# Decoder attention: the third bank of turned probabilities goes from VectorE to ScalarE

## The chip, the cores and the metric

The kernel runs on one core of a Trainium2 chip. The metric is the device time of one execution in microseconds: 2270.2 us is the median of three (2270.14 to 2271.83). The profile is of one more execution, which took 2272.19 us; its instructions span 2270.4 us.

## The reference

Two blocks of a decoder over 512 tokens of width 1024, in float32. The change lies in the attention of the second block, whose core is, with 16 heads in 2 groups of 8 and 64 columns a head:

```
scale = HEAD_DIM ** -0.5
s = einsum('bghqd,bgnd->bghqn', q_c, k_cmp) * scale - slopes * dist     # 31 compressed keys
o_cmp = softmax(s) @ v_cmp
s = einsum('bghqd,bgqkld->bghqkl', q_c, ks) * scale - slopes * dist     # selected blocks
o_slc = softmax(s) @ vs
s = einsum('bghqd,bgmd->bghqm', q_c, kw) * scale - slopes * dist        # window of 512
o_win = softmax(s) @ vw
o = g_c[0] * o_cmp + g_c[1] * o_slc + g_c[2] * o_win                    # gates, per token and head
out = o @ w_out
```

With 512 tokens all 8 blocks of 64 are selected and the window of 512 reaches over all earlier tokens, so the second and the third softmax are both causal over all keys and differ in their keys and values.

## The kernel before, in words

All matrices stand as 128 partitions by columns. Weights are streamed from memory, and each product of float32 values is made of three matmuls on rounded high and low parts (`products`, L288 to L290). They are most of the kernel. The attention (`attend_tensor`, `attend_scalar`, `attend_vector`) is one stage of some 210 us out of 2270.

The attention works on **pairs** of heads, one of each group, 8 pairs in all. A turn of its loop holds 2 pairs, and there are 4 turns. A pair is 5 items, in the list `ITEMS`: item 0 the compressed keys, items 1 and 2 the selected keys for group 0 and 1, items 3 and 4 the window keys for group 0 and 1. In a turn the second pair's items are numbered 5 to 9. For each item but the compressed one:

- TensorE makes the scores (`scores_tensor`, L1965) in banks 2, 3 and 4 of PSUM (the accumulators).
- VectorE reads them, adds the bias by distance and finds the extreme value of each row (`read_vector`, L2155), four pieces of 512, 384, 128 and 256 columns into `Pr`.
- ScalarE takes the exponential of each piece with its row sum (`exp_scalar`, L2067).
- VectorE inverts the sums, multiplies with the gate and scales the probabilities (`scale_vector`, L2190, L2193, L2198).
- TensorE turns (transposes) them, ten 128x128 blocks into banks 5, 6 and 1 (`turn_probs_tensor`, L1991), and raises `turned` after each bank.
- The three banks are evicted into `PT[g]`, 512, 512 and 256 columns: banks 5 and 1 by ScalarE (`evict_scalar`, L2081, `pT_act`), bank 6 by VectorE (`evict_vector`, L2166, `pT_dve`).
- After the second group's item (2 and 4) TensorE multiplies values with both `PT`, 16 matmuls (`weigh_tensor`, L2010), here called the **weighing**. It waits for the evictions. So does the next turning, since it writes the same banks.

In between TensorE makes the query projection of the pair after next (`pair_tensor`, with `products`), two of eight chunks at a time. When it is complete, ScalarE evicts its high parts (`q_scalar`, L2090, `q_high`) and VectorE makes its low parts (`q_vector`, L2129, `q_ready`). This stands behind item 1's eviction on ScalarE and behind item 2's scaling on VectorE, once a pair, except where no pair follows. GpSimd splits one weight tile a pair meanwhile (L233, L253).

Each engine runs its own instructions strictly in the order in which the functions below write them. ScalarE's step n is: exponentials of item n+2, eviction of item n, then `q_scalar` at items 1 and 6. VectorE's step n is: scores of item n+2, eviction of item n, scaling of item n+1, then `q_vector`. TensorE's step n is: turning of item n, a part of a projection, scores of item n+3, weighing.

Of the kernel before, what the change touches and what calls it, by code (L numbers as in the profile page):

```python
# [136 lines left out]
def program(nc, t, out):  # L137

    with ExitStack() as ctx:
# [4 lines left out]
        def at(name, offset, cols, dt=F32, parts=P):  # L144
            return nc.alloc_sbuf_tensor_at(name, [parts, cols], dt, offset=base + offset)
# [37 lines left out]
        bank = [ctx.enter_context(nc.psum_tensor(f"bank{i}", [P, 512], F32)) for i in range(8)]  # L183

        def sem(name):
            return ctx.enter_context(nc.semaphore(name))
# [22 lines left out]
        def wait_apart(engine, semaphore, value):  # L209


            engine.wait_ge(semaphore, value)
            engine.sem_inc(passed, 1)
# [1596 lines left out]
        def kv_vector(dve, order):  # L1810
# [58 lines left out]
            for i in range(2):  # L1869
# [27 lines left out]
        PR_OF = [0, 1, 2, 0, 1, 2, 0, 1]  # L1897
        PT = [at("PT0", 42 * KB, PCOLS), at("PT1", behind_r, PCOLS)]
        (alibi_ready, c_scored, scores_read, piece_read, c_maxed, c_shifted, probs_done, c_summed, c_turned, cT_ready, scored,
         turned, pT_act, pT_dve, inverse, weight_ready, probs_scaled, q_high, q_ready, pair_done, y_high, y_low) = (  # L1900
            sem(n) for n in ("alibi_ready c_scored scores_read piece_read c_maxed c_shifted probs_done c_summed c_turned cT_ready "
                             "scored turned pT_act pT_dve inverse weight_ready probs_scaled q_high q_ready pair_done y_high y_low").split())
        q_units, q_tiles = seg_a.unit0 + 7, seg_a.tile0 + 7
        TURNS = NQ // 2
        Q_PARTS = {2: (0, 2), 3: (2, 4), 4: (4, 6), 0: (6, 8)}
# [1 line left out]
        def item(idx):  # L1907

            return ITEMS[idx % N_ITEMS]

        def nth(i, idx):

            return i * N_ITEMS + idx

        def s_nth(i, idx):

            return i * 8 + (idx // N_ITEMS * 8 + sum(1 for it in ITEMS[:idx % N_ITEMS] if it[1]))

        def c_nth(i, idx):

            return i * 2 + (idx // N_ITEMS * 2 + sum(1 for it in ITEMS[:idx % N_ITEMS] if not it[1]))

        def probs(idx):
            return Pr[PR_OF[sum(1 for it in ITEMS[:idx % N_ITEMS] if it[1])]]
# [44 lines left out]
        def turn_probs_tensor(pe, i, idx):  # L1969

            _, r, g = item(idx)
            if r:
                pe.wait_ge(probs_scaled, nth(i, idx) + 1)
            else:
                wait_apart(pe, probs_scaled, nth(i, idx) + 1)
                for b in range(NB):
                    mm = nc.tensor.transpose(bank[5][0:64, b * P:(b + 1) * P], Pc[:, b * 64:(b + 1) * 64], ident)
                mm.then_inc(c_turned, 1)
                return
            if g:  # L1980
                pe.wait_ge(pT_dve, s_nth(i, idx))
                pe.wait_ge(pT_act, s_nth(i, idx) * 2)
            elif r == 1:
                pe.wait_ge(cT_ready, c_nth(i, idx))
            P_ = probs(idx)
            for pieces, (first, _), into in zip(TURNED, GROUPS, (bank[5], bank[6], bank[1])):
                for kb, col in pieces:
                    for b in range(kb, NB):
                        at0 = col - first + (b - kb) * P
                        c = WHERE[b] + kb * P  # L1990
                        mm = nc.tensor.transpose(into[:, at0:at0 + P], P_[:, c:c + P], ident)  # L1991
                mm.then_inc(turned, 1)

        def weigh_tensor(pe, i, idx):

            j, r, g = item(idx)
            if r == 0:
                pe.wait_ge(y_low, i * 2 + (j + 1))
                pe.wait_ge(cT_ready, c_nth(i, idx) + 1)
                nc.tensor.matmul(bank[7][:, :], v_cmp[:, :], PcT[:, :], start=True, stop=False)  # L2000
                return
            if g == 0:
                return
            m = s_nth(i, idx)
            pe.wait_ge(pT_dve, m + 1)
            pe.wait_ge(pT_act, m * 2 + 2)
            for kb in range(NB):
                col = KEYS_AT[kb]
                for e in range(2):
                    mm = nc.tensor.matmul(bank[7][HALVES[e], kb * P:], v_tok[r - 1][:, kb * P + 64 * e:kb * P + 64 * e + 64],  # L2010
                                          PT[e][:, col:col + (NB - kb) * P], start=False, stop=r == 2 and kb == NB - 1)
            if r == 2:
                mm.then_inc(pair_done, 1)
# [57 lines left out]
        def evict_scalar(act, i, idx):  # L2071

            _, r, g = item(idx)
            if r == 0:
                act.wait_ge(c_turned, c_nth(i, idx) + 1)
                nc.scalar.activation(PcT[:, :], bank[5][0:64, :], ACT.Identity).then_inc(cT_ready, 1)
                return
            for n, source_bank in ((0, bank[5]), (2, bank[1])):
                act.wait_ge(turned, s_nth(i, idx) * 3 + (n + 1))
                first, end = GROUPS[n]  # L2080
                nc.scalar.activation(PT[g][:, first:end], source_bank[:, 0:end - first], ACT.Identity).then_inc(pT_act, 1)  # L2081
# [50 lines left out]
        def read_vector(dve, i, idx):  # L2132


            _, r, g = item(idx)
            V = nc.vector
            if r == 0:
                c = c_nth(i, idx)
                dve.wait_ge(alibi_ready, c * 4 + 2)
                dve.wait_ge(c_scored, c + 1)  # L2140
                V.tensor_tensor(Pc[:, :], bank[2][:, 0:2 * P], alibi_c[:, :], ALU.add).then_inc(scores_read, 1)
                dve.wait_ge(scores_read, nth(i, idx) + 2)
                by_block = Pc[:, :].rearrange("p (b n) -> p b n", n=32)
                V.tensor_reduce(c_max, by_block, AX.X, ALU.max).then_inc(c_maxed, 1)
                dve.wait_ge(c_maxed, c + 1)
                V.tensor_tensor(by_block, by_block, over_columns(c_max, 32), ALU.subtract).then_inc(c_shifted, 1)
                return
            if r == 1:
                dve.wait_ge(alibi_ready, c_nth(i, idx) * 4 + (g - 1))
            P_ = probs(idx)  # L2150
            for n, pieces in enumerate(PIECES):
                wait_apart(dve, scored, s_nth(i, idx) * 3 + (n + 1))
                for b, col in pieces:
                    at0 = col - GROUPS[n][0]
                    ins = V.tensor_tensor_reduce(P_[:, col:col + (b + 1) * P], bank[2 + n][:, at0:at0 + (b + 1) * P],  # L2155
                                                 alibi[g][:, (3 - b) * P:], -KEY_SCALE, 3.0e38, ALU.add, ALU.min,
                                                 stat(idx, 0)[:, b:b + 1])
                ins.then_inc(piece_read if n < 2 else scores_read, 1)

        def evict_vector(dve, i, idx):  # L2160

            _, r, g = item(idx)
            if r:
                m = s_nth(i, idx)
                dve.wait_ge(turned, m * 3 + 2)
                nc.vector.tensor_copy(PT[g][:, 512:1024], bank[6][:, :]).then_inc(pT_dve, 1)  # L2166

        def scale_vector(dve, i, idx):

            j, r, g = item(idx)  # L2170
# [37 lines left out]
        def attend_vector(dve):  # L2208
            nc.vector.sem_inc(scores_read, 1)
            nc.vector.sem_inc(y_low, 1)  # L2210
            nc.vector.sem_inc(tile_taken, NQ)
            read_vector(dve, 0, 0)
            read_vector(dve, 0, 1)
            scale_vector(dve, 0, 0)

            def turn(i):
                for n in range(N_ITEMS):
                    if exists(i, n + 2):
                        read_vector(dve, i, n + 2)
                    evict_vector(dve, i, n)  # L2220
                    if exists(i, n + 1):
                        scale_vector(dve, i, n + 1)
                    if n % PER_PAIR == 1 and exists(i, n + PER_PAIR - 1):
                        q_vector(dve, *((i, 1) if n < PER_PAIR else (i + 1, 0)))
                    if n == PER_PAIR:
                        y_vector(dve, i, 0)
                    if n == 0 and not (isinstance(i, int) and i == 0):
                        y_vector(dve, i - 1, 1)

            turn(0)  # L2230
            with dve.Fori(1, TURNS - 1) as i:
                turn(i)
            turn(TURNS - 1)
            y_vector(dve, TURNS - 1, 1)
# [224 lines left out]
```

## Time and profile before

| | |
|---|---|
| median of three runs | 2270.2 us (2270.14 to 2271.83) |
| profiled execution | 2272.19 us, its span 2270.4 us |
| TensorE busy | 2129.6 us, 94% |
| VectorE busy | 1186.0 us, 52% |
| ScalarE busy | 851.5 us, 38% |
| GpSimd busy | 778.0 us, 34% |
| mean granted TensorE clock | 0.972 of full speed |
| chain of work that ended last | TensorE 79%, VectorE 11%, issue 5%, ScalarE 4% |

Whole-kernel shares say little on the attention. There the rows by stage, by line and in order of time have to be read: which instruction on TensorE waits, for whom, and what that engine did just before.

### The profile page before, as it was taken

The page shows a single profiled execution, that of the slowest core. Times are in us where ns is not written, and L with a number is a line of the kernel's source. Part 1 is how long each engine was busy: PE and PEld are TensorE (multiplying, and loading weights), DVE is VectorE, ACT ScalarE, POOL GpSimd, SP SyncE. Part 2 cuts the span into 40 slices and gives each one's busy share as a digit, 9 for nine tenths or more (in the row PEclk, how much of TensorE's full clock was granted, in tenths as well). Part 3 has the DMA queues.
Part 4 walks back from the last instruction along what each step waited for, and adds up shares of the span by engine and source line. Part 5 has one row for each costly group of instructions (what it writes and reads, how often), then busy time and mean ns, then how long its engine had stood idle before and what let it go on. Part 6 is the DMA issues. An engine that isn't in the chain of part 4 may idle for free.

```text
span 2270.4 us, 32867 instructions
## 1 busy us (share of the span) xinstructions
PE 2129.6 (94%) x11670; PEld 1714.6 (76%) x11670; DVE 1186.0 (52%) x1862; ACT 851.5 (38%) x1516; POOL 778.0 (34%) x336
## 2 busy tenths in 40 slices
PE   3889999989899999899979999999999989999997
PEld 2768788768688888768757888888877667888886
DVE  6476977762533332289964333323677864333323
ACT  3333442433432332275543232322366643323221
POOL 2632332404244444300114444444411114444442
PEclk8989999999999999999989999999999999999999
DMA  3311211203233332211113333322200003333332
GB/s 120 102 56 42 63 38 40 64 2 120 66 101 92 101 102 98 70 56 47 56 28 93 93 101 92 129 93 87 71 20 19 28 22 92 100 92 101 102 102 75
DMA packets 43652, 168.98 MB, mean 74 GB/s; under 512 B 4848, under 2 KB 4912, under 8 KB 43056
## 3 DMA queue, kind: packets, MB, share of 16 engines
q1 hardware_dynamic: 43056, 163.59, 23.6%
q10 hardware_dynamic: 512, 4.24, 0.5%
q8 instruction: 56, 0.92, 0.2%
q14 instruction: 28, 0.23, 0.0%
HBM read 165.72 MB, written 2.10 MB: 74 GB/s over the span
## 4 chain that ended last, share of the span: by engine, by line
PE 79%; DVE 11%; issue 5%; ACT 4%; POOL 1%; DMA 1%; DVEq 0%; ACTq 0%; POOLq 0%; SPq 0%
PE bank L288 21%; PE bank L289 21%; PE bank L290 21%; PE bank L745 2%; PE bank L2010 2%; PE bank L1965 1%; DVE act_q L1019 1%; POOL WL L253 1%; PE bank L1507 1%; PE bank L1509 1%; PE bank L1508 1%; ACT Pr L2067 1%; PE bank L1991 1%; DVE ACC L415 1%; PE bank L314 1%
## 5 line engine op out<-in xcount | busy, mean ns | idle before, releaser
L253 POOL TENSOR_TENSOR WL<-raw,WR 128x1024 fp32r<-128x1024 f32 (+2 forms) x274 | 713.0, 2602 | 1031.1 <-ACT WR L249 1026.5
L288 PE MATMUL bank<-XR,WR 128*128 128x512 f32 x1528 | 616.6, 404 | 28.6 <-DVE XL L444 19.5
L290 PE MATMUL bank<-XR,WL 128*128 128x512 f32 x1528 | 597.4, 391 | 0.0
L289 PE MATMUL bank<-XL,WR 128*128 128x512 f32 x1528 | 597.1, 391 | 0.0
L249 ACT ACTIVATE WR<-raw 128x1024 fp32r<-128x1024 f32 (+2 forms) x230 | 256.0, 1114 | 781.3 <-PE bank L290 772.2
L288 PEld LDWEIGHTS bank<-XR,WR 128*128 128x128 f32 x1528 | 288.5, 189 | 103.8 <-issue 33.6
L288 PE MATMUL bank<-MR,WR 128*128 128x512 f32 (+1 forms) x856 | 338.2, 395 | 13.6 <-DVE ML L1678 6.1
L289 PEld LDWEIGHTS bank<-XL,WR 128*128 128x128 f32 x1528 | 288.7, 189 | 65.2 <-issue 8.3
L290 PEld LDWEIGHTS bank<-XR,WL 128*128 128x128 f32 x1528 | 288.1, 189 | 61.0
L289 PE MATMUL bank<-ML,WR 128*128 128x512 f32 (+1 forms) x856 | 333.1, 389 | 0.0
L290 PE MATMUL bank<-MR,WL 128*128 128x512 f32 (+1 forms) x856 | 333.0, 389 | 0.0
L233 POOL CAST WR<-raw 128x1024 fp32r<-128x1024 f32 (+1 forms) x58 | 64.9, 1118 | 436.9 <-PE bank L290 377.1
L1463 DVE TENSOR_TENSOR f_up<-bank,R 128x512 f32<-128x512 f32 x66 | 45.6, 692 | 306.0 <-PE bank L290 306.0
L288 PEld LDWEIGHTS bank<-MR,WR 128*128 128x128 f32 x856 | 163.3, 191 | 52.0 <-issue 12.1
L290 PEld LDWEIGHTS bank<-MR,WL 128*128 128x128 f32 x856 | 163.6, 191 | 33.0
L289 PEld LDWEIGHTS bank<-ML,WR 128*128 128x128 f32 x856 | 163.9, 191 | 31.1 <-issue 0.2
L415 DVE TENSOR_TENSOR ACC<-ACC,SQ 128x512 f32<-128x512 f32 (+1 forms) x56 | 89.2, 1593 | 145.1 <-ACT SQ L404 143.8
L1468 DVE TENSOR_TENSOR ML<-f_mid,MR 128x512 f32 x66 | 123.9, 1877 | 64.5 <-ACT MR L1445 64.5
L1405 DVE TENSOR_TENSOR hT<-bank,hT 128x512 f32 (+1 forms) x24 | 16.6, 692 | 161.0 <-PE bank L290 161.0
L1461 DVE TENSOR_TENSOR f_gate<-bank,R 128x512 f32<-128x512 f32 x66 | 45.6, 692 | 88.4 <-PE bank L290 73.0
L2067 ACT ACTIVATE Pr<-Pr,stats 128x512 f32<-128x512 f32 (+3 forms) x128 | 70.4, 551 | 44.1 <-DVE stats L2155 44.0
L444 DVE SCALAR_TENSOR_TENSOR XL<-hT,params,XR (+1 forms) x40 | 69.3, 1733 | 33.3 <-ACT XR L440 33.3
(303 smaller groups left out, 2451.9 us busy)
## 6 DMA issues: line engine op xcount, KB each, us to landing
raw<-w SPq DMA_DIRECT2D x224, 512.0 KB, 3.5
raw<-w SPq DMA_DIRECT2D x48, 704.0 KB, 4.1
raw<-w SPq DMA_DIRECT2D x16, 384.0 KB, 3.1
hT<-xT SPq DMA_DIRECT2D x1, 2048.0 KB, 7.8
hT<-xT ACTq DMA_DIRECT2D x1, 2048.0 KB, 8.0
out<-Y SPq DMA_DIRECT2D x8, 256.0 KB, 2.0
memT<-memT ACTq DMA_DIRECT2D x1, 1024.0 KB, 7.5
phi<-phi ACTq DMA_DIRECT2D x1, 1024.0 KB, 6.4
```

What stands on the lines that cost most here:

```text
L233: nc.gpsimd.tensor_copy(WR[:, here], raw[:, here]).then_inc(high_split, 1)
L249: nc.scalar.activation(WR[:, here], raw[:, here], ACT.Identity).then_inc(high_ahead, 1)
L253: nc.gpsimd.tensor_tensor(WL[:, here], raw[:, here], WR[:, here].bitcast(F32), ALU.subtract).then_inc(weight_split, 1)
L288: nc.tensor.matmul(into, wr, xr(k0 + k), start=start, stop=False)
L289: nc.tensor.matmul(into, wr, xl(k0 + k), start=False, stop=False)
L290: mm = nc.tensor.matmul(into, wl, xr(k0 + k), start=False, stop=stop)
L415: nc.vector.tensor_tensor(ACC[:, 0:width], ACC[:, 0:width], SQ[:, parity * SEQ:parity * SEQ + width], ALU.add).then_inc(summed, 1)
L444: nc.vector.scalar_tensor_tensor(dst, src, gain, high.bitcast(F32), ALU.mult, ALU.subtract).then_inc(input_ready, 1)
L1461: nc.vector.tensor_tensor(f_gate[:, :], bank_of(seg, 2 * p)[:, :], R[:, :], ALU.mult).then_inc(tile_taken, 1)
L1463: nc.vector.tensor_tensor(f_up[:, :], bank_of(seg, 2 * p + 1)[:, :], R[:, :], ALU.mult).then_inc(tile_taken, 1)
L1468: nc.vector.tensor_tensor(cols(ML, n), f_mid[:, :], cols(MR, n).bitcast(F32), ALU.subtract).then_inc(mid_low, 1)
L2067: ins = nc.scalar.activation(here, here, ACT.Exp, bias=stat(idx, 0)[:, b:b + 1], scale=-1.0, accum_out=stat(idx, 1)[:, b:b + 1])
```

## The change

ScalarE evicts all three banks, in the order 5, 6, 1, and counts 3 in `pT_act` for an item. VectorE's copy of bank 6 and its semaphore are gone. TensorE waits for `pT_act` alone. Nothing else moves.

```diff
@@ turn_probs_tensor
             if g:
-                pe.wait_ge(pT_dve, s_nth(i, idx))
-                pe.wait_ge(pT_act, s_nth(i, idx) * 2)
+                pe.wait_ge(pT_act, s_nth(i, idx) * 3)
@@ weigh_tensor
             m = s_nth(i, idx)
-            pe.wait_ge(pT_dve, m + 1)
-            pe.wait_ge(pT_act, m * 2 + 2)
+            pe.wait_ge(pT_act, m * 3 + 3)
@@ evict_scalar
-            for n, source_bank in ((0, bank[5]), (2, bank[1])):
+            for n, source_bank in ((0, bank[5]), (1, bank[6]), (2, bank[1])):
                 act.wait_ge(turned, s_nth(i, idx) * 3 + (n + 1))
                 first, end = GROUPS[n]
                 nc.scalar.activation(PT[g][:, first:end], source_bank[:, 0:end - first], ACT.Identity).then_inc(pT_act, 1)
@@
-        def evict_vector(dve, i, idx):
-            _, r, g = item(idx)
-            if r:
-                m = s_nth(i, idx)
-                dve.wait_ge(turned, m * 3 + 2)
-                nc.vector.tensor_copy(PT[g][:, 512:1024], bank[6][:, :]).then_inc(pT_dve, 1)
@@ attend_vector
                         read_vector(dve, i, n + 2)
-                    evict_vector(dve, i, n)
                     if exists(i, n + 1):
                         scale_vector(dve, i, n + 1)
```

ScalarE's order from item 1's eviction to item 2's, before (`PT_185` is `PT[0]`, `PT_186` is `PT[1]`, `Q_S_173` and `Q_S_174` are the next pair's queries, `Pr_182` holds item 4):

```order
L2067 ACTIVATE Pr_184,stats<-Pr_184,stats 128x256 [waits scores_read]
L2081 ACTIVATE PT_185<-bank 128x512 [waits turned]
L2081 ACTIVATE PT_185<-bank 128x256 [waits turned]
L2090 ACTIVATE Q_S_173<-bank 64x512 [waits unit_done]
L2090 ACTIVATE Q_S_174<-bank 64x512
L2067 ACTIVATE Pr_182,stats<-Pr_182,stats 128x512 [waits piece_read]
L2067 ACTIVATE Pr_182,stats<-Pr_182,stats 128x384 [waits piece_read]
L2067 ACTIVATE Pr_182,stats<-Pr_182,stats 128x128
L2067 ACTIVATE Pr_182,stats<-Pr_182,stats 128x256 [waits scores_read]
L2081 ACTIVATE PT_186<-bank 128x512 [waits turned]
L2081 ACTIVATE PT_186<-bank 128x256 [waits turned]
```

The same place after the change:

```order
L2065 ACTIVATE Pr_184,stats<-Pr_184,stats 128x256 [waits scores_read]
L2079 ACTIVATE PT_185<-bank 128x512 [waits turned] x2
L2079 ACTIVATE PT_185<-bank 128x256 [waits turned]
L2088 ACTIVATE Q_S_173<-bank 64x512 [waits unit_done]
L2088 ACTIVATE Q_S_174<-bank 64x512
L2065 ACTIVATE Pr_182,stats<-Pr_182,stats 128x512 [waits piece_read]
L2065 ACTIVATE Pr_182,stats<-Pr_182,stats 128x384 [waits piece_read]
L2065 ACTIVATE Pr_182,stats<-Pr_182,stats 128x128
L2065 ACTIVATE Pr_182,stats<-Pr_182,stats 128x256 [waits scores_read]
L2079 ACTIVATE PT_186<-bank 128x512 [waits turned] x2
L2079 ACTIVATE PT_186<-bank 128x256 [waits turned]
```

One more eviction of 512 columns stands ahead of the queries, and a second one ahead of the last eviction that the weighing needs. VectorE's order over the same stretch, before, from the last scores of item 3 to the low parts of the queries:

```order
L2155 ISA Pr_184,stats<-bank,alibi_175 128x256
L2155 ISA stats 128x1
L2166 COPY PT_185<-bank 128x512
L2190 RECIPROCAL stats<-stats 128x4
L2193 TENSOR_TENSOR stats<-stats,gates 128x4
L2198 TENSOR_SCALAR Pr_183<-Pr_183,stats 128x512
L2198 TENSOR_SCALAR Pr_183<-Pr_183,stats 128x384
L2198 TENSOR_SCALAR Pr_183<-Pr_183,stats 128x128
L2198 TENSOR_SCALAR Pr_183<-Pr_183,stats 128x256
L2129 TENSOR_TENSOR Q_S_173<-bank,Q_S_173 64x512
L2129 TENSOR_TENSOR Q_S_174<-bank,Q_S_174 64x512
```

After, the copy is gone and all else stands as it stood:

```order
L2153 ISA Pr_184,stats<-bank,alibi_175 128x256
L2153 ISA stats 128x1
L2180 RECIPROCAL stats<-stats 128x4
L2183 TENSOR_TENSOR stats<-stats,gates 128x4
L2188 TENSOR_SCALAR Pr_183<-Pr_183,stats 128x512
L2188 TENSOR_SCALAR Pr_183<-Pr_183,stats 128x384
L2188 TENSOR_SCALAR Pr_183<-Pr_183,stats 128x128
L2188 TENSOR_SCALAR Pr_183<-Pr_183,stats 128x256
L2127 TENSOR_TENSOR Q_S_173<-bank,Q_S_173 64x512
L2127 TENSOR_TENSOR Q_S_174<-bank,Q_S_174 64x512
```

## Rows read from the trace of the kernel before

**Rows 1.** Busy time of one turn: stretch, length, PE, PEld, DVE, ACT, POOL, clock, DMA.
```profile
1664.35:1715.52 51.17, 50.00 (x300) 37.15 (x301) 40.67 (x143) 33.79 (x99) 6.87 (x4) 0.97 0.07 21
```

**Rows 2.** Chain in order of time, 1715 to 1767 us: start, duration, what.
```profile
1731.49 1.00 PE bank L1965 x6
...
1736.54 0.59 DVE Q_S L2129
...
1741.03 0.88 ACT PT L2081 x2
...
1741.95 2.37 PE bank L2010 x16
```

**Rows 3.** ScalarE in order of time: start, duration, line, what [idle before, for whom].
```profile
1735.08 0.58 ACT L2081 ACTIVATE PT<-bank 128x512 f32<-128x512 f32 x1
...
1735.56 0.36 ACT L2081 ACTIVATE PT<-bank 128x256 f32<-128x256 f32 x1
...
1735.82 0.58 ACT L2090 ACTIVATE Q_S<-bank 64x512 fp32r<-64x512 f32 x1
...
1738.71 0.72 ACT L2067 ACTIVATE Pr<-Pr,stats 128x512 f32<-128x512 f32 x1 [1.69 <-DVE stats L2155]
```

**Rows 4.** VectorE and GpSimd over the same stretch, in order of time.
```profile
1732.78 2.39 POOL L253 TENSOR_TENSOR WL<-raw,WR 128x1024 fp32r<-128x1024 f32 x1
...
1733.79 0.69 DVE L2166 COPY PT<-bank 128x512 f32<-128x512 f32 x1
...
1734.72 0.48 DVE L2193 TENSOR_TENSOR stats<-stats,gates 128x4 f32<-128x4 f32 x1 [0.15 <-DVE stats L2190]
...
1735.23 1.28 DVE L2198 TENSOR_SCALAR Pr<-Pr,stats 128x512 f32<-128x512 f32 x4
...
1740.55 0.17 DVE L2193 TENSOR_TENSOR stats<-stats,gates 128x4 f32<-128x4 f32 x1 [0.15 <-DVE stats L2190]
```

**Rows 5.** TensorE in order of time: item 2's turning, compressed scores, item 4's weighing.
```profile
1736.74 1.31 PE L1991 MATMUL bank<-table,Pr 128*128 128x128 f32 x10 [0.22 <-DVE Pr L2198]
...
1739.77 1.96 PE L1957 MATMUL bank<-KC,Q_S 128*128 128x32 f32 x16
...
1751.90 2.38 PE L2010 MATMUL bank<-PT,v_tok 128*64 128x512 f32 x16
```

**Rows 6.** ScalarE, item 4's eviction, in order of time.
```profile
1750.62 0.84 ACT L2081 ACTIVATE PT<-bank 128x512 f32<-128x512 f32 x2
```

**Rows 7.** Each pair's first weighing as a stretch, TensorE alone: length, busy, clock, DMA.
```profile
1664.35:1668.42 4.07, 4.07 (x17) 0.58 0.00 0
1690.79:1693.16 2.37, 2.37 (x17) 1.00 0.00 0
1715.52:1719.58 4.06, 4.06 (x17) 0.58 0.01 2
1741.95:1744.33 2.38, 2.38 (x17) 1.00 0.00 0
...
1817.89:1821.95 4.06, 4.06 (x17) 0.58 0.01 2
1840.77:1843.14 2.37, 2.37 (x17) 1.00 0.00 0
```

**Rows 8.** The last pair and the end of the attention, in order of time.
```profile
1825.36 1.31 PE L1991 MATMUL bank<-table,Pr 128*128 128x128 f32 x10 [0.88 <-DVE Pr L2198]
...
1840.77 2.37 PE L2010 MATMUL bank<-PT,v_tok 128*64 128x512 f32 x16 [2.06 <-ACT PT L2081]
...
1843.77 1.04 ACT L2081 ACTIVATE PT<-bank 128x512 f32<-128x512 f32 x2 [3.14 <-PE bank L1991]
...
1846.54 1.31 PE L1991 MATMUL bank<-table,Pr 128*128 128x128 f32 x10 [2.15 <-DVE Pr L2198]
1847.23 1.04 ACT L2081 ACTIVATE PT<-bank 128x512 f32<-128x512 f32 x2 [2.43 <-PE bank L1991]
...
1848.41 2.38 PE L2010 MATMUL bank<-PT,v_tok 128*64 128x512 f32 x16 [0.56 <-DVE PT L2166]
```

More of the change, by code:

```diff
@@ L1899, in program @@
         (alibi_ready, c_scored, scores_read, piece_read, c_maxed, c_shifted, probs_done, c_summed, c_turned, cT_ready, scored,
-         turned, pT_act, pT_dve, inverse, weight_ready, probs_scaled, q_high, q_ready, pair_done, y_high, y_low) = (
+         turned, pT_act, inverse, weight_ready, probs_scaled, q_high, q_ready, pair_done, y_high, y_low) = (
             sem(n) for n in ("alibi_ready c_scored scores_read piece_read c_maxed c_shifted probs_done c_summed c_turned cT_ready "
-                             "scored turned pT_act pT_dve inverse weight_ready probs_scaled q_high q_ready pair_done y_high y_low").split())
+                             "scored turned pT_act inverse weight_ready probs_scaled q_high q_ready pair_done y_high y_low").split())
         q_units, q_tiles = seg_a.unit0 + 7, seg_a.tile0 + 7
```

## The prediction

> **What bounds the kernel now.** I read the page's chain by line first, then the stretches of the attention, its chain in order of time, the engines in order of time around TensorE's waits, and last the clock of each weighing. Over the kernel TensorE carries 79% of the chain, and the change touches none of its matmuls, so only the attention counts. One turn there takes 51.17 us [rows 1], TensorE busy for 50.00, VectorE for 40.67, ScalarE for 33.79. By these shares ScalarE has room and the work seems to go to the right place.
>
> The order of time says otherwise. From each pair's first weighing until item 3's scores of the next pair the chain stays on TensorE. From there [rows 2] it leaves TensorE for 9.5 us a pair: scores at 1731.49 + 1.00 = 1732.49, then VectorE, the low parts of the queries at 1736.54, item 4's read on VectorE, item 4's exponentials on ScalarE, item 2's evictions at 1741.03, and the weighing at 1741.95. TensorE has small work meanwhile, but the weighing starts 0.04 after the last eviction. This stretch comes once a pair, in seven pairs; in the last turn's second pair no queries are made and it runs otherwise.
>
> **Part one: the first added eviction, ahead of the queries.** ScalarE starts item 1's eviction of 512 columns at 1735.08 and the one of 256 at 1735.56 [rows 3]: from start to start a 512-column eviction costs 0.48 us. One more moves both query evictions by 0.48. The first ends now at 1735.82 + 0.58 = 1736.40, and VectorE starts its low part at 1736.54 [rows 2, 3], 0.14 later, which is about a handover. VectorE's own scaling ends at 1735.23 + 1.28 = 1736.51 [rows 4], so both engines are ready there at once: no slack on either side. After the change VectorE waits for ScalarE, until 1737.02. The low parts, the read of item 4 and ScalarE's exponential of it (1738.71, where ScalarE now idles 1.69 for VectorE [rows 3]) all come 0.48 later.
>
> **Part two: the copy taken from VectorE.** It frees 0.60 us there, 1733.79 to L2190 at 1734.39 by the order of time. In this stretch that buys nothing, since the queries wait for ScalarE anyway. It may not even come to pass: the small product L2193 of 4 columns runs 0.48 here, from 1734.72 to 1735.20, and 0.17 at 1740.55; beside the first one GpSimd's L253 runs from 1732.78 to 1735.17 [rows 4]. It ends as GpSimd ends. Started 0.60 earlier it would most likely end at the same 1735.2. The Trainium skill has this as a rule (SBUF — State Buffer, section "SBUF: two separate sides"): VectorE, when an instruction reads two SBUF tensors, and GpSimd share one pair of ports as an exclusive lock, and the one that comes second is held for the other's whole instruction. By that rule the copy's removal is worth nothing before the queries even if ScalarE were free, which speaks against the third rival below; the three places at which I read both rows agree.
>
> The copy of item 2 lies beside ScalarE's exponentials and is not on the path. Item 2's turning, at 1736.74, waits for item 2's scaling and not for an eviction [rows 5]; item 1's evictions end then at 1735.56 + 0.36 + 0.48 = 1736.40, still before it. So the turning stays where it is.
>
> **Part three: the second added eviction, ahead of the weighing.** Item 2's evictions start 0.48 later by part one and hold one more of 0.48. The weighing comes 0.96 later. Seven pairs: 7 x 0.96 = 6.7 us. Bounds: if the low parts had slack that I don't see, 0.48 a pair, 3.4; if each eviction cost its full 0.58, 1.16 a pair, 8.1. I take 6.7, since start to start is what the order of time shows for this very instruction.
>
> Item 3's evictions end some 2 us before the next turning and hide theirs. Item 4's end at 1750.62 + 0.84 = 1751.46 against a weighing at 1751.90 [rows 5, 6]: 0.48 more fills the 0.44, so up to 0.1 a pair shows. I count 0 for it, since VectorE reads item 6's scores about 0.08 earlier there. The 0.7 is kept for the upper end.
>
> **Part four: the end of the attention, where VectorE's relief does count.** In the last turn TensorE has no projection to fill with. Item 9's turning waits 2.15 us for VectorE's scaling [rows 8], which stood behind the copy of item 8, and that had waited for the turning of item 8. Without the copy the scaling is done long before, and the turning waits for ScalarE: start 1843.77, three evictions in 1.04 + 0.29 = 1.33 (the 1.04 holds a wait of some 0.19 for the last bank), so it starts at 1845.17 instead of 1846.54, 1.37 earlier. The same 1.33 for item 9 ends at 1847.23 - 1.37 + 1.33 = 1847.19, and the last weighing starts at 1847.28 instead of 1848.41: 1.1 us gained. Ahead of it the last pair's items gain some from VectorE (the turning at 1825.36 waits 0.88 for a scaling behind a copy) and lose three times 0.48 on ScalarE; worked through the weighing of 1840.77 comes 0.4 earlier, between 0 and 1.0. Together -1.5, between -1.1 and -2.1.
>
> **Part five: TensorE's clock.** The sixteen matmuls of a pair's first weighing take 2.37 us at the full 2.4 GHz, and 4.06 us in the first pair of each turn, whose granted clock is 0.58, a mean of the two levels of 1.2 and 2.4 GHz [rows 7]. That costs 1.69 each, four times of eight. What TensorE did just before is the same in both: the last projection matmuls, sixteen of only 32 columns each [rows 5], a wait for ScalarE. The second pairs escape, though their stretch looks the same. After the change it is 0.96 longer with no work added, in every pair: I expect the fall in all seven, three more, 3 x 1.69 = 5.1. Bounds: no more falls, 0; the eighth pair too, 6.8. In the other direction the shifted pairs could lose all four, -6.8; nothing in the rows speaks for it, as a longer thin stretch can't be busier.
>
> The Trainium skill (TensorE: Matmul & The Clock Gate, section "A second HAM failure mode: psum-queue depth-cycling") says that short idles between groups of matmuls, round after round through the banks, are enough to make the clock go back and forth. This trace agrees in four pairs of eight. By the rule the longer stretch falls in each pair; if it doesn't hold for so small a change, the first rival is left.
>
> **Sum.** 6.7 - 1.5 + 5.1 = +10.3. Falls are not placed alike in each run, and a fall that begins before the weighing costs less than 1.69: I take 0.5 off and say +9.8. The profiled execution took 2272.19 (span 2270.4), so its counterpart is 2282.0; it lies 2.0 above the median of the runs, and the median comes to 2280.0.
>
> **Rivals.**
> First, waits only: the clock falls in four pairs as before. For it: the second pairs kept their clock in all four turns. Against: their stretch grows by a tenth and more. 6.7 - 1.5 = +5.2, 2275.4.
>
> Second, ScalarE's additions are hidden and the tail's gain is all, or a partial effect cancels it: for example the falls drop by four while the waits come as worked out, 6.7 - 1.5 - 6.8 = -1.6, 2268.6. For it: the places of the pairs do shift. It is no change by the measure here: 0.2%, 4.5 us, is what a measurement of this kernel can tell, so faster begins at 2265.7 and slower at 2274.7.
>
> Third, on the other side, faster: VectorE is the engine that the stretch waits for. It is busy nearly without a gap from 1732 to 1742, ScalarE idles 1.69 for it, and its copy costs 0.69 against ScalarE's 0.58 for the same bank [rows 3, 4]. If the query evictions were early enough, 0.60 x 7 = 4.2 would go, and the tail's 1.5 with it: -5.7, 2264.5. It decides from the point where the first query eviction ends 0.6 before VectorE's scaling; the rows show 0.11, and L2193 is held by GpSimd. Against it stands also that the weighing waits for ScalarE's evictions, not for VectorE's.
>
> That the change does nothing can't be: the instructions move in the order.
>
> **How the numbers follow.** Forecast (waits and three or so more falls) 57%, waits only 20%, no change by the second rival 14%, faster by the third 9%. The waits-only case straddles the border of 2274.7 and gives a quarter to no change: slower 72%, same 19%, faster 9%. Range: below, it takes in most of the waits-only case, whose low end is 3.4 - 1.5, and part of the second rival: 2271. Above, 8.1 + 0.7 - 1.1 + 6.8 = 14.5 gives 2284.7: 2285. The likeliest case alone has 2277 to 2284.
>
> **What would show it.** In the profile after: ScalarE's three evictions of item 1 and the first query eviction 0.48 later after the exponentials; VectorE idle before the low parts of the queries, waiting for ScalarE (it has no such idle now); L2193 beside GpSimd still ending with it; the weighing 0.96 later after item 3's scores; a period of some 54.7 us for a turn instead of 51.17; 4 us in nearly all first weighings; item 9's turning waiting for ScalarE about 1.4 earlier after item 8's. I am wrong if the low parts start where VectorE's scaling ends, if the turn stays at 51 us, or if the weighings keep 2.37 us.

## The result, and the profile after

The changed kernel takes 2279.1 us (2277.5 to 2281.0, six runs) against 2270.2 of the kernel before, measured beside it: 1.0035 times as long, with a 95% interval of 1.0025 to 1.0046. That is 8.9 us slower, where 9.8 was forecast. The profiled execution took 2277.48 us, its span 2275.7.

The busy times and the chain's shares by engine on the page after:

```profile
PE 2131.0 (94%) x11670; PEld 1713.2 (75%) x11670; DVE 1171.5 (51%) x1830; ACT 866.2 (38%) x1548; POOL 777.7 (34%) x336
...
PE 79%; DVE 10%; ACT 5%; issue 5%; POOL 1%; DMA 1%; DVEq 0%; ACTq 0%; POOLq 0%; SPq 0%
```

VectorE lost 14.5 us of work and ScalarE took up 14.7. TensorE runs the same 11670 matmuls. It was busy 1.4 us longer in all: 4.4 longer in the attention, 3.0 less in the code ahead of it, which is unchanged and varies from one execution to the next. The shares show nothing of where 8.9 us went.

The turn that answers to [rows 1]: stretch, length, then PE, PEld, DVE, ACT, POOL, clock, DMA.

```profile
1716.26:1770.79 54.53, 51.63 (x300) 37.45 (x300) 37.20 (x135) 37.44 (x107) 6.86 (x4) 0.94 0.07 19
```

It is 54.53 us where it was 51.17, with the same TensorE instructions; the clock fell from 0.97 to 0.94, and TensorE's busy time rose by 1.63, which is one more slow weighing (the kernel before has one in a turn, this one two). The rest of the 3.36 is waiting, 1.73 or twice 0.87.

TensorE alone in the eight first weighings, one row a pair (stretch, length, PE, clock, then DMA), against [rows 7]:

```profile
1662.00:1665.84 3.84, 3.84 (x17) 0.61 0.00 0
1689.07:1693.03 3.96, 3.96 (x17) 0.59 0.00 0
1716.26:1720.28 4.02, 4.02 (x17) 0.58 0.00 0
1743.51:1747.56 4.05, 4.05 (x17) 0.58 0.00 0
1770.79:1774.85 4.06, 4.06 (x17) 0.58 0.00 0
1798.09:1802.15 4.06, 4.06 (x17) 0.58 0.00 0
1825.38:1829.45 4.07, 4.07 (x17) 0.58 0.00 0
1847.11:1849.48 2.37, 2.37 (x17) 1.00 0.00 0
```

Seven of seven have a clock near 0.6, not every second one. The eighth, where no queries are made and the stretch runs otherwise, kept 1.00 as before. The first ones are a little shorter than the later ones because their slow stretch begins earlier: in the wait of 0.72 us just ahead, in which TensorE does nothing, the granted clock is 0.71 for the first pair, 0.88 and 0.96 for the next two, and 1.00 from the fourth on.

The chain of waits after, at the same weighing as in [rows 2]:

```profile
1742.10 1.37 ACT PT L2079 x3
1743.51 4.04 PE bank L2008 x16
```

Three evictions of item 2 instead of two end 0.04 before it.

The stretch ahead of that weighing in order of time, all engines, against [rows 3] and [rows 4] (start, duration, engine, line, what, and in brackets the idle time before it and for whom):

```profile
1732.02 1.44 PE L1965 MATMUL bank<-KS,Q_S 128*128 128x512 f32 x8
...
1733.48 2.38 POOL L253 TENSOR_TENSOR WL<-raw,WR 128x1024 fp32r<-128x1024 f32 x1
...
1734.80 1.08 DVE L2183 TENSOR_TENSOR stats<-stats,gates 128x4 f32<-128x4 f32 x1
...
1735.77 1.32 ACT L2079 ACTIVATE PT<-bank 128x512 f32<-128x512 f32 x3
...
1735.92 1.27 DVE L2188 TENSOR_SCALAR Pr<-Pr,stats 128x512 f32<-128x512 f32 x4
...
1736.99 0.58 ACT L2088 ACTIVATE Q_S<-bank 64x512 fp32r<-64x512 f32 x1
...
1737.61 1.41 DVE L2127 TENSOR_TENSOR Q_S<-bank,Q_S 64x512 fp32r<-64x512 f32 x2 [0.42 <-ACT Q_S L2088]
...
1739.15 0.49 PE L288 MATMUL bank<-MR,WR 128*128 128x512 f32 x1 [0.51 <-DVE Q_S L2127]
...
1740.84 1.96 PE L1957 MATMUL bank<-KC,Q_S 128*128 128x32 f32 x16
...
1741.02 0.17 DVE L2183 TENSOR_TENSOR stats<-stats,gates 128x4 f32<-128x4 f32 x1
...
1742.10 1.36 ACT L2079 ACTIVATE PT<-bank 128x512 f32<-128x512 f32 x3
...
1743.51 1.12 PE L2008 MATMUL bank<-PT,v_tok 128*64 128x512 f32 x2 [0.72 <-ACT PT L2079]
```

From item 3's scores, 1732.02, all is measured: the low parts of the queries start 5.59 later (before: 5.21) and the weighing 11.49 later (before: 10.62). The small product L2183 started early, after the missing copy, and was held for 1.08 until 1735.88, where GpSimd's instruction ends at 1733.48 + 2.38 = 1735.86. VectorE's scaling therefore ends 5.17 after the scores, where it ended 5.18 after them before the change: the missing copy bought nothing. VectorE then waits 0.42 for ScalarE's query eviction; it had no such wait.

The end of the attention after, the same view, against [rows 8]:

```profile
1847.11 2.38 PE L2008 MATMUL bank<-PT,v_tok 128*64 128x512 f32 x16 [2.04 <-ACT PT L2079]
...
1849.41 1.31 PE L1990 MATMUL bank<-table,Pr 128*128 128x128 f32 x10
...
1850.10 1.36 ACT L2079 ACTIVATE PT<-bank 128x512 f32<-128x512 f32 x3 [3.05 <-PE bank L1990]
1851.61 1.28 PE L1990 MATMUL bank<-table,Pr 128*128 128x128 f32 x10 [0.89 <-ACT PT L2079]
...
1853.69 2.37 PE L2008 MATMUL bank<-PT,v_tok 128*64 128x512 f32 x16 [0.80 <-ACT PT L2079]
```

Item 9's turning waits 0.89 for ScalarE instead of 2.15 for VectorE, and the last weighing follows the eighth first one by 6.58 us instead of 7.64.

**Where the 8.9 us are.** From the first compressed scores to the end of the last weighing the attention grew by 8.45 us, 209.84 to 218.29. By terms: waits 7 x 0.87 = 6.1; slow weighings, by their durations above 2.37, 11.5 against 6.8, so 4.7; the end, from the seventh first weighing on, -2.2. The sum is 8.6. The two profiled executions differ by only 5.3, since the unchanged code ahead of the attention took 3.2 us less in the one of after (the attention began at 1637.77 instead of 1640.95): the medians are the measure.

### The profile page after: what moved, and what is told of

Its sections match the earlier page's. It is cut to its first block, busy times and chain, and to the rows that moved or that the text cites. A ratio compares the mean times of both kernels' runs of the same rounds, so it can differ in the third digit from the quotient of the medians.

```text
span 2275.7 us, 32853 instructions
## 1 busy us (share of the span) xinstructions
PE 2131.0 (94%) x11670; PEld 1713.2 (75%) x11670; DVE 1171.5 (51%) x1830; ACT 866.2 (38%) x1548; POOL 777.7 (34%) x336
## 4 chain that ended last, share of the span: by engine, by line
PE 79%; DVE 10%; ACT 5%; issue 5%; POOL 1%; DMA 1%; DVEq 0%; ACTq 0%; POOLq 0%; SPq 0%
PE bank L288 21%; PE bank L290 21%; PE bank L289 21%; PE bank L745 2%; PE bank L2008 2%; ACT Pr L2065 1%; ACT PT L2079 1%; PE bank L1965 1%; DVE act_q L1019 1%; POOL WL L253 1%; PE bank L1507 1%; PE bank L1508 1%; PE bank L1509 1%; PE bank L1990 1%; DVE ACC L415 1%
```

## The experiments

All are compared with the kernel before, run on the same chip. In the tables **low** is the start of the queries' low parts and **W** that of the weighing, both from item 3's scores in us; **slow** is how many of the seven first weighings took over 3 us; **W1 to W7** is the time between the starts of the first and the seventh of them. These four are read from one profiled execution of each kernel, the median from all its runs, and the ratio is to runs of the kernel before taken beside it (medians 2270.7 for e1 to e4, 2271.3 for e5 to e8, 2271.0 for e9 to e12). **W** is that of the first six pairs. The seventh lies in the last turn, where TensorE waits 2.0 to 2.4 us before the compressed scores in every kernel but e9, and there it comes later in some: 12.01 in e1, 12.33 in e2, 13.61 in e4, 13.89 in e6, 12.40 in e10, 11.66 in e11.

### Each eviction by itself, and neither of the two

The kernel before, where `BY_VECTOR` names the items whose bank 6 VectorE keeps (item numbers 5 to 9 are the second pair's):

```diff
+        BY_VECTOR = [1, 6]      # e2: [2, 7]   e3: [1, 2, 6, 7]   e12: [1, 2, 3, 4, 6, 7]
-            for n, source_bank in ((0, bank[5]), (2, bank[1])):
+            for n, source_bank in ((0, bank[5]), (1, bank[6]), (2, bank[1])):
+                if n == 1 and idx in BY_VECTOR:
+                    continue
@@ evict_vector
-            if r:
+            if r and idx in BY_VECTOR:
```

with the counts that TensorE waits for made to fit.

VectorE keeps items 1 and 6, so that only the second added eviction stands in the stretch:

> VectorE evicts bank 6 for items 1 and 6 only (the eviction ahead of the queries), ScalarE for all others. Theory: ScalarE's two additions cost apart and add up, 0.38 us by the queries and 0.49 by item 2's evictions. So the queries' low parts start 5.2 us after item 3's scores, as before the change (5.6 after it), and the weighing 11.1 after them (before 10.6, after 11.5). Seven times 0.49, less 1.1 to 2.2 at the end of the attention, and one or two clock falls more than before's four: 2273 us. Rival, the last eviction is the whole loss and the queries are hidden: weighing still 11.5 after the scores, about 2279.

VectorE keeps items 2 and 7, so that only the first one does:

> VectorE evicts bank 6 for items 2 and 7 only (the eviction ahead of the weighing), ScalarE for all others. Theory: only the queries' 0.38 us is left: low parts 5.6 us after item 3's scores, weighing 11.0 after them, one fall more than before's four: 2272 us. Rival, the queries are the whole loss: weighing at 11.5, about 2279. Rival, they cost nothing: weighing at 10.6, 2268.

VectorE keeps both:

> VectorE evicts bank 6 for items 1, 2, 6 and 7, ScalarE for items 3, 4, 8 and 9. Theory: nothing is lost in the stretch before the weighing (10.6 us after item 3's scores, four falls, turns of 51.2 us), and the end of the attention keeps its gain of 1.1 us by items 8 and 9, with up to 1.1 more in the last turn: 2268 to 2269 us, just below before. Rival, ScalarE's evictions of items 3 and 4 cost too: weighing of item 4 later, turns of 51.5 us or more, 2270 us or more.

VectorE keeps all but items 8 and 9:

> ScalarE evicts bank 6 for items 8 and 9 only, VectorE for all others. Theory: only the gain at the very end is left, 1.1 us from the last pair's first weighing to the last one (6.6 us instead of 7.6), and the stretch from the seventh pair's to the last pair's first weighing is 22.9 us as before: 2269.5 us. Rival, items 8 and 9 also give the 1.2 us between those two weighings: 21.7 us there, 2268.5 us.

| kernel | low | W | slow | W1 to W7 | median us | ratio [95%] |
|---|---|---|---|---|---|---|
| before | 5.21 | 10.62 | 4 | 153.54 | 2270.2 | |
| after | 5.59 | 11.49 | 7 | 163.38 | 2279.1 | 1.0035 [1.0025, 1.0046] |
| e1 | 5.21 | 11.11 | 6 | 160.56 | 2277.3 | 1.0024 [1.0015, 1.0034] |
| e2 | 5.59 | 11.00 | 6 | 160.38 | 2274.2 | 1.0015 [1.0005, 1.0024] |
| e3 | 5.21 | 10.62 | 4 | 153.51 | 2268.9 | 0.9989 [0.9979, 0.9998] |
| e12 | 5.20 | 10.62 | 4 | 153.52 | 2269.6 | 0.9992 [0.9983, 1.0002] |

The two evictions add up: 0.49 for the second alone, 0.38 for the first alone, 0.87 together. Each alone already makes six weighings slow, which I had put at one or two more than four. So both took longer than expected, e1 2277.3 where I had 2273, e2 2274.2 where I had 2272, though their low parts and weighings lie where the theory put them and not where the rivals did. In both, the seventh pair's compressed scores also ran at a granted clock near 0.5 (some 3.5 us instead of 1.93). Why e1 and e2 are 3.1 apart when their waits differ by only 0.11 a pair, these two profiles don't show; single runs of e2 lie between 2271.0 and 2276.6. e2's stretch in order of time, item 3's scores at 1730.97, as an instance:

```profile
1736.56 1.41 DVE L2142 TENSOR_TENSOR Q_S<-bank,Q_S 64x512 fp32r<-64x512 f32 x2 [0.42 <-ACT Q_S L2103]
...
1741.05 0.87 ACT L2094 ACTIVATE PT<-bank 128x512 f32<-128x512 f32 x2
...
1741.97 0.65 PE L2021 MATMUL bank<-PT,v_tok 128*64 128x512 f32 x2 [0.23 <-ACT PT L2094]
```

Here only two evictions stand ahead of the weighing, but the low parts already wait 0.42. The wait that the low parts have after the change is there in full, with less than half of the delay of the weighing (0.38 of 0.87).

e3 and e12 leave the loop as before (low, W, slow and W1 to W7 within 0.03). They part the gain at the end: in e12 (items 8 and 9 on ScalarE) the last weighing comes 1.06 earlier than before and the last pair nothing; in e3, with items 3 and 4 too, the last pair is 1.17 shorter, 22.88 to 21.71. So both gains are ScalarE's evictions of the window items. e12 can't be told from no change, and e3 hardly.

### Is VectorE what the stretch waits for?

The third rival had VectorE as the engine that the stretch waits for. In the changed kernel GpSimd's low part is held back until the queries' low parts are done, so that nothing stands in VectorE's way (the new loop around it is left out here):

```diff
+                        if j >= 9:
+                            pool.wait_ge(q_ready, 2 * (j - 8))
                         low_unit(seg, unit % 2)
```

> The changed kernel, where GpSimd makes the low part of a query weight only after VectorE's low parts of the queries, so that it no longer runs beside VectorE's scaling. Theory: the small product before the scaling takes 0.17 us instead of 1.08 and the scaling ends some 0.9 us earlier, but the queries still wait for ScalarE, so their low parts stay 5.6 us and the weighing 11.5 us after item 3's scores, and the time stays at 2279 us. Rival, VectorE held by GpSimd is what the stretch waits for: low parts at 5.2 or less, weighing at 11.0, 2275 us or less.

The stretch in order of time, item 3's scores at 1730.38:

```profile
1733.16 0.17 DVE L2183 TENSOR_TENSOR stats<-stats,gates 128x4 f32<-128x4 f32 x1
...
1735.98 1.41 DVE L2127 TENSOR_TENSOR Q_S<-bank,Q_S 64x512 fp32r<-64x512 f32 x2 [1.34 <-ACT Q_S L2088]
...
1737.54 2.38 POOL L253 TENSOR_TENSOR WL<-raw,WR 128x1024 fp32r<-128x1024 f32 x1 [5.79 <-DVE Q_S L2127]
...
1739.38 0.56 DVE L2183 TENSOR_TENSOR stats<-stats,gates 128x4 f32<-128x4 f32 x1
...
1741.88 3.59 PE L2008 MATMUL bank<-PT,v_tok 128*64 128x512 f32 x10 [0.72 <-ACT PT L2079]
```

The product takes 0.17 again and VectorE is free 1.34 before it can begin the low parts. The weighing still comes 1741.88 - 1730.38 = 11.50 after the scores, and the kernel takes 2279.3 us, 1.0041 [1.0026, 1.0055] of before. The edit reached five of the seven pairs. In the sixth and seventh GpSimd still ran beside the product, which took 1.08 and 1.18, and the low parts and the weighing lie at the same places there (5.58 and 5.59, 11.49 and 11.50). The relief of VectorE is real and buys nothing: the low parts wait for ScalarE's query eviction, not for VectorE's scaling. Behind them VectorE's own work, the low parts and the read of item 4, is on the chain in both kernels. The held product has only moved to the next place beside GpSimd (0.56).

### The clock: matmuls in the wait

Matmuls of 128x512 whose results nobody reads, between the compressed scores and the weighing, in the changed kernel (e4 four, e11 two) and in the kernel before (e6 four):

```diff
                         scores_tensor(pe, i, n + 3)
+                        if n % PER_PAIR == 2:
+                            for _ in range(4):        # e11: 2
+                                nc.tensor.matmul(bank[3][:, :], KS[0][0][0][:, 0:P], KS[0][0][0][:, :], start=True, stop=True)
```

> The changed kernel with four matmuls of 128x512 more in each pair, whose result nobody reads, between the compressed scores and the first weighing, where TensorE only waits. Theory: the clock falls because this stretch is thin; with 0.9 us of dense matmuls in it the falls are fewer, at best none of seven: first weighings of 2.4 us instead of 4.0, the waits of 0.87 a pair stay. From 2279 down by 7 x 1.64 to 2268 us, or to 2273 if half the falls stay. Rival, the falls don't depend on what TensorE does there: weighings stay at 4.0 us, 2279 us or, if the four matmuls delay the weighing, 2281.

> The kernel before with the same four matmuls of 128x512 in each pair, between the compressed scores and the first weighing. Theory: four clock falls of 1.69 us go, and since TensorE waits there only 0.2 us for the evictions, the weighing comes some 0.7 us later in seven pairs: 2270.5 - 6.8 + 4.9 = 2269 us. Rival, the falls are not those of this stretch: they stay, and the time rises to 2275 us.

> The changed kernel with two instead of four matmuls added in the stretch. They fit into the wait, so the weighing stays 11.5 us after item 3's scores, and the time is 2279 us less 1.6 for each fall that goes. Theory: two matmuls (0.45 us) take away some falls and not all: 2270 to 2275 us. Rival, it takes the whole 0.9 us of before: no fall goes, 2279 us.

| kernel | W | slow | W1 to W7 | median us | ratio [95%] |
|---|---|---|---|---|---|
| e4, after + four | 11.71 | 1 | 156.91 | 2273.5 | 1.0006 [0.9996, 1.0015] |
| e11, after + two | 11.49 | 1 | 153.85 | 2270.0 | 0.9995 [0.9986, 1.0004] |
| e6, before + four | 11.34 | 1 | 155.24 | 2274.4 | 1.0011 [1.0002, 1.0021] |

e11 is the clean one. TensorE in order of time, and the turn by busy times:

```profile
1738.34 1.96 PE L1957 MATMUL bank<-KC,Q_S 128*128 128x32 f32 x16
...
1740.15 0.71 PE L2035 MATMUL bank<-KS 128*128 128x512 f32 x2
...
1741.01 2.37 PE L2008 MATMUL bank<-PT,v_tok 128*64 128x512 f32 x16 [0.15 <-ACT PT L2082]
```
```profile
1715.40:1766.63 51.23, 49.44 (x305) 36.99 (x305) 37.21 (x135) 37.44 (x107) 6.86 (x4) 1.00 0.07 21
```

The two matmuls fit into the wait of 0.72 (0.15 is left), the weighing keeps its place at 11.49, and it takes 2.37 us at a clock of 1.00. W1 to W7 is 9.53 shorter than after: six slow weighings gone, 1.6 each, and the kernel is 9.1 us faster, level with before, though the low parts and the weighing lie as late as after the change. So the slow weighings are clock, and what they added is nearly half of what the change costs in the loop.

The idle time right ahead of the weighing doesn't decide it alone: it is 0.23 in e2, where six weighings are slow, and 0.35 in e10 below, where none of those six is.

e4 had 2273.5 where I had put 2268 to 2273. All six weighings are fast, but four matmuls are longer than the wait and move each by 0.22, and the seventh pair's comes 2.1 later and is still slow (3.77).

My expectation for e6 failed: I had 2269 and it took 2274.4. Its first six weighings are fast, where three were slow before, but four matmuls are too long for the shorter wait there; the weighing came 0.72 later in each of the six. In the last turn the seventh pair's weighing came 3.19 later and was still slow (3.06), and the eighth, fast before, took 4.06. That turn, TensorE in order of time, shows what the matmuls don't mend:

```profile
1814.79 3.56 PE L1957 MATMUL bank<-KC,Q_S 128*128 128x32 f32 x16 [1.98 <-DVE stats L2158]
...
1818.19 2.05 PE L2037 MATMUL bank<-KS 128*128 128x512 f32 x4
1820.17 3.06 PE L2010 MATMUL bank<-PT,v_tok 128*64 128x512 f32 x16
```

With no projection to make, TensorE idles 1.98 before the compressed scores; sixteen matmuls of 32 columns take 3.56 where they take 1.93 in the kernel before, at a granted clock of 0.50 instead of 1.00, so the clock was down ahead of the filling.

### Real work in the stretch

The query projection is made in eight chunks. One more of them is put right after item 2's turning, and one fewer after item 0's, in e3 (e7), in before (e8) and in after (e10):

```diff
-        Q_PARTS = {2: (0, 2), 3: (2, 4), 4: (4, 6), 0: (6, 8)}
+        Q_PARTS = {2: (0, 3), 3: (3, 5), 4: (5, 7), 0: (7, 8)}
```

> VectorE evicts bank 6 for items 1, 2, 6 and 7 and ScalarE for the others, and one of the eight chunks of each query projection is moved from the stretch bound by TensorE (after item 0) into the one where it waits (item 2: three chunks instead of two). Theory: nothing is added, 0.68 us less TensorE work stands outside the stretch and at most 0.25 us more inside it, so 0.4 to 0.7 us a pair go, 3 to 5 us in seven, and the fuller stretch has no more than four falls: 2262 to 2266 us. Rival, TensorE's own order is the bound in the stretch too: the weighing comes 0.68 us later, 2269 us.

> The kernel before with that chunk moved alone. Theory: the same gain of 3 to 5 us, without the gain of some 2 us at the end of the attention that ScalarE's evictions of items 3, 4, 8 and 9 give: 2264 to 2268 us. Rival as for the run beside it: 2271 us.

> The changed kernel with the same chunk of each query projection moved into the stretch (three chunks at item 2). Theory: the stretch waits 0.87 us a pair more than before, so 0.68 us of real work fit without delay: weighing still 11.5 us after item 3's scores, a pair 0.68 shorter, seven times 4.8 us; and the fuller stretch loses at least half of the seven falls: 2279 - 4.8 - 6 = 2268 us. Rival, the falls stay: 2274 us.

e9 is e7, and in the last turn, which has no projection, eight unread matmuls stand before the compressed scores:

```diff
+                    if isinstance(i, int) and i == TURNS - 1 and n % PER_PAIR == 2:
+                        pe.wait_ge(q_ready, 4 * TURNS)
+                        for _ in range(8):
+                            nc.tensor.matmul(bank[0][:, :], KS[0][0][0][:, 0:P], KS[0][0][0][:, :], start=True, stop=True)
```

> As the run with the moved chunk and VectorE at items 1, 2, 6 and 7 (2263.7 us), and in the last turn, which has no projections, eight matmuls of 128x512 into a bank nobody reads, after the turning of items 2 and 7, where TensorE waits some 2 us. Theory: its two first weighings of 4.5 and 4.0 us go back to 2.4, less what the added matmuls delay: 2260 to 2262 us. Rival, the eight matmuls delay the scores by more than the falls cost: 2264 us or more.

| kernel | low | W | slow | W1 to W7 | median us | ratio [95%] |
|---|---|---|---|---|---|---|
| e10, after + chunk | 5.58 | 11.49 | 1 | 150.38 | 2265.4 | 0.9975 [0.9965, 0.9984] |
| e8, before + chunk | 5.21 | 10.70 | 1 | 144.93 | 2265.5 | 0.9978 [0.9968, 0.9987] |
| e7, e3 + chunk | 5.20 | 10.70 | 1 | 145.02 | 2263.7 | 0.9964 [0.9950, 0.9978] |
| e9, e7 + last turn | 5.21 | 10.70 | 0 | 144.79 | 2258.6 | 0.9944 [0.9931, 0.9958] |

The chunk costs the weighing at most 0.08 and is gone elsewhere: a turn of e11, also without slow weighings there, takes 51.23, and one of e10 49.83, which is 0.70 less a pair, the whole chunk. (W1 to W7 is only 3.47 shorter, because the seventh pair's weighing comes 0.91 later in e10: its compressed scores ran at a clock of 0.50 and took 3.57.) I had expected half of the falls to go and 2268 us; six went, and it took 2265.4. A turn of e10 by busy times, and TensorE before its weighing:

```profile
1712.92:1762.75 49.83, 47.74 (x301) 36.70 (x301) 37.23 (x135) 37.41 (x107) 6.86 (x4) 1.00 0.07 21
```
```profile
1735.64 1.85 PE L1957 MATMUL bank<-KC,Q_S 128*128 128x32 f32 x16
...
1737.84 0.65 PE L2008 MATMUL bank<-PT,v_tok 128*64 128x512 f32 x2 [0.35 <-ACT PT L2079]
```

With the change in place and the weighing as late as it makes it, the turn is 49.83 at full clock, shorter than before. That e8 and e10 take the same time isn't because the waits are gone: from W1 to W7 e10 is 5.45 longer. e8 gives that back in its last turn, where the change's gain at the end is missing and the seventh and the very last weighing are slow (4.54 and 4.19).

e7's slow weighings stood in the last turn alone (4.54, and 3.98 for the eighth); in e9 they are gone, and it took 2258.6 where I had 2260 to 2262. e9's chain there, the first weighing of each of the two pairs, and its turn by busy times:

```profile
1806.68 2.37 PE bank L2021 x16
...
1826.74 2.38 PE bank L2021 x16
```
```profile
1710.15:1758.41 48.26, 47.60 (x301) 36.68 (x301) 38.42 (x138) 35.48 (x103) 6.88 (x4) 1.00 0.07 22
```

e9 beats both kernels: 12.4 us under the 2271.0 of before beside it, and 20.5 under the changed kernel. Without unread matmuls e7 is the best.

## Why the prediction was right

**Part one, the added eviction ahead of the queries** (0.48 foreseen): the place and the cause were right, the size 0.38. The first query eviction ends at 1736.99 + 0.58 = 1737.57 and VectorE starts at 1737.61. So the handover takes 0.04 here, not the 0.14 that stood between the two before; I had read a slack of 0.10 as part of the handover, though my own rows had it: the eviction ended 0.11 before VectorE's scaling (1736.40 and 1736.51), so VectorE was the later of the two by that much. e2 shows the 0.38 alone.

**Part two, the copy's removal worth nothing there**: shown twice. L2183 ended with GpSimd's instruction in all seven pairs, as the Trainium skill's rule has it (SBUF — State Buffer, section "SBUF: two separate sides"), and e5 took that hold away in five of them without any gain.

**Part three, the second eviction** (0.48 foreseen): 0.49 in e1, and the sum of both 0.87, not 0.96. For seven pairs 6.1 instead of 6.7. Item 2's turning stayed hidden. What I had not foreseen is that TensorE's projection waits 0.51 for the low parts (at 1739.15), which only moves idle time within the stretch.

**Part four, the end** (-1.5 foreseen): -2.2. The last weighing was right, 1.06 against 1.1 (item 9's turning came 1.27 earlier after item 8's, not 1.37). The last pair's gain was mis-sized: 1.15 against 0.4, beyond its bound of 1.0. I had let three times 0.48 on ScalarE eat most of what the copies give back; e3 and e12 show that the copies of items 3 and 4 carry the gain.

**Part five, the clock** (5.1 less 0.5 foreseen): 4.7 by the durations, and seven of seven fell. The count was right and the direction of the reasoning too, but a longer stretch isn't a full account: with 0.38 or 0.49 more instead of 0.87, six already fall, and the fourth pair doesn't. e11 shows that the clock is the cause of the 1.6 us each and not, for instance, a late operand: same place of the weighing, 2.37. The 0.5 off was needed; the first two falls take only 3.84 and 3.96, since they begin before the weighing.

The Trainium skill tells of short idles between groups of matmuls that make the clock go back and forth (TensorE: Matmul & The Clock Gate, section "A second HAM failure mode: psum-queue depth-cycling"). Seven pairs of seven are in keeping with it, but so were four of eight: it doesn't say in which rounds the clock falls, so the step in the prediction from it to a fall in each pair was mine.

**The rivals.** Waits only: refuted by the weighings' durations. The clock regained: nothing regained in the loop; the second rival's partial gain at the end was in the sum already. VectorE as the bound: refuted by e5. Of the terms, 6.7 came to 6.1, -1.5 to -2.2, 4.6 to 4.7: 9.8 became 8.6, with 8.9 between the medians. The two terms that were off erred to the same side, so the sum owes nothing to errors that cancel. The number of falls is the part that could have gone otherwise, by 1.6 us each.

What stays open: why the kernel before loses its clock in every second pair and not in the other. The records of the two pairs show no difference that I can name, and no experiment aimed at it. The same holds for the fourth pair of e1 and e2. Not settled either is what it is in the stretch that brings the clock down, the small matmuls or the idle times: every edit that kept the clock up added matmuls to the stretch and shortened an idle time at once.

## What to carry to other kernels

Shares of busy time pointed the wrong way: ScalarE was 38% busy and still the engine that the one stretch waited for at the queries and at the weighing, so count what stands in order on an engine between the last thing it waits for and the one that waits for it. Where TensorE's durations jump between two values for one line, read the granted clock of that line alone, and ask what thin work stood ahead of it; moving real matmuls into that place repaid more (2265.4 with the change) than undoing the change. Filling should fit into the wait: two matmuls cost nothing in the first six pairs, four moved the weighing.

## What the hardware showed that I had not expected

- A product of 4 columns on VectorE took 1.08 us (0.17 elsewhere) and ended 0.02 us after GpSimd's 2.38 us instruction.
- Two matmuls of 128x512 in a wait of 0.72 us took away six falls of the clock of about 1.6 us each. Between item 3's scores and those weighings the kernel without them has no idle time on TensorE over 0.72; the work right ahead of that wait was sixteen matmuls of 32 columns.
- With every pair slow, the loop settles into a fixed beat: first weighings at 1770.79, 1798.09 and 1825.38, 27.30 and 27.29 us apart, and the duration of the first weighings creeps from 3.84 to 4.07 over the seven.
- An eviction of 512 columns costs 0.49 us where it stands in a row with others and 0.58 by its own duration, and VectorE took up ScalarE's result 0.04 us after its recorded end.
